# The split weights' slots, each begun at another byte phase of a partition's 512 bytes

## The reference

```python
x = x + 0.5 * swiglu_ffn(rmsnorm(x, ffn1_norm), ffn1_w_in, ffn1_w_out)   # 2048 -> 2*5504 -> 2048
h = rmsnorm(x, mix_norm)
qa, ka, va, qb, kb, vb, f_pre = split(h @ w_in)                          # 2048 -> 6152
out_a = dilated_attention(rmsnorm(qa), rmsnorm(ka), va, rel_bias_table)  # 8 heads of 128
out_b = forgetting_attention(rmsnorm(qb), rmsnorm(kb), vb, log_f)        # 8 heads of 128
x = x + concat(out_a, out_b) @ w_out
x = x + 0.5 * swiglu_ffn(rmsnorm(x, ffn2_norm), ffn2_w_in, ffn2_w_out)

def swiglu_ffn(x, w_in, w_out):
    gate, up = split(x @ w_in, 2)
    return (silu(gate) * up) @ w_out
```

## Time and profile before

| | |
|---|---|
| median of 2 runs | 1900.01 us (1899.78 to 1900.24) |
| the profiled execution | 1897.12 us |
| its span, first to last instruction | 1895.3 us |
| mean granted TensorE clock | 0.995 of full speed |
| PE busy | 1858.9 us, 98% of the span |
| weight load (PEld) busy | 1545.2 us, 82% |
| DVE busy | 946.6 us, 50% |
| ACT busy | 818.2 us, 43% |
| DMA | 343.70 MB read, 183 GB/s over the span |

### The profile page before, as it was taken

How to read it: one execution, slowest core, us unless ns; L and a number is a source line. 1 busy time by engine, 2 the same in 40 slices (tenths; PEclk the granted TensorE clock), 3 DMA queues, 4 the chain that set the end, 5 groups by cost and what they waited for, 6 DMA issues and landing times.

```text
span 1895.3 us, 20376 instructions
## 1 busy us (share of the span) xinstructions
PE 1858.9 (98%) x8470; PEld 1545.2 (82%) x8470; DVE 946.6 (50%) x1051; ACT 818.2 (43%) x971; POOL 26.9 (1%) x37
## 2 busy tenths in 40 slices
PE   6999999999999999999999999999999999999999
PEld 5888888888988888877777788888888888988887
DVE  4444444454544554365555555545444444444443
ACT  5444444444434444344444445444444444433332
POOL 1000000000000000000000000000000000000000
PEclk9999999999999999899999999999999999999999
DMA  6655555555655557344454455555655555556553
GB/s 225 213 197 181 197 185 192 190 187 172 206 194 186 181 200 241 108 137 156 145 166 155 164 170 177 180 198 179 198 180 199 182 195 180 192 185 210 202 202 116
DMA packets 175643, 347.13 MB, mean 183 GB/s; under 512 B 5808, under 2 KB 14064, under 8 KB 175424
## 3 DMA queue, kind: packets, MB, share of 16 engines
q1 hardware_dynamic: 172304, 337.92, 54.1%
q10 hardware_dynamic: 2080, 3.94, 0.6%
q0 software_dynamic: 1168, 3.97, 0.5%
HBM read 343.70 MB, written 3.68 MB: 183 GB/s over the span
## 4 chain that ended last, share of the span: by engine, by line
PE 93%; DVE 3%; ACT 2%; issue 1%; DMA 1%; ACTq 0%; DVEq 0%
PE acc L248 30%; PE acc L250 30%; PE acc L249 29%; ACT whi L458 2%; DVE wlo L676 1%; PE aux L275 1%; DMA x<-x 1%; PE aux L265 1%; PE aux L327 0%; DVE act_f L782 0%; PE aux L378 0%; PE aux L370 0%; PE aux L369 0%; PE aux L340 0%; PE aux L339 0%
## 5 line engine op out<-in xcount | busy, mean ns | idle before, releaser
L676 DVE TENSOR_TENSOR wlo<-raw,whi 128x1024 fp32r<-128x1024 f32 (+1 forms) x656 | 790.8, 1206 | 913.5 <-ACT whi L458 911.7
L458 ACT ACTIVATE whi<-raw 128x1024 fp32r<-128x1024 f32 (+1 forms) x656 | 684.6, 1044 | 1036.6 <-PE acc L250 1036.6
L248 PE MATMUL acc<-whi,xs 128*128 128x512 f32 (+1 forms) x1792 | 700.1, 391 | 3.7 <-DVE wlo L676 3.6
L250 PE MATMUL acc<-whi,xs 128*128 128x512 f32 (+1 forms) x1792 | 692.3, 386 | 0.0
L249 PE MATMUL acc<-wlo,xs 128*128 128x512 f32 (+1 forms) x1792 | 691.8, 386 | 0.0
L248 PEld LDWEIGHTS acc<-whi,xs 128*128 128x128 f32 x1792 | 337.4, 188 | 68.4 <-issue 5.1
L250 PEld LDWEIGHTS acc<-whi,xs 128*128 128x128 f32 x1792 | 337.3, 188 | 66.3
L249 PEld LDWEIGHTS acc<-wlo,xs 128*128 128x128 f32 x1792 | 337.6, 188 | 63.7
L248 PE MATMUL acc<-whi,act 128*128 128x512 f32 x688 | 268.1, 390 | 0.0
L250 PE MATMUL acc<-whi,act 128*128 128x512 f32 x688 | 267.7, 389 | 0.0
L249 PE MATMUL acc<-wlo,act 128*128 128x512 f32 x688 | 267.7, 389 | 0.0
(11 more groups left out here) (116 smaller groups left out, 519.4 us busy)
## 6 DMA issues: line engine op xcount, KB each, us to landing
raw<-ffn_w_in SPq DMA_DIRECT2D x160, 1024.0 KB, 4.9
raw<-ffn_w_out SPq DMA_DIRECT2D x80, 1024.0 KB, 4.9
raw<-w_in SPq DMA_DIRECT2D x48, 1024.0 KB, 5.0
raw<-w_out SPq DMA_DIRECT2D x16, 1024.0 KB, 4.9
raw<-ffn_w_in SPq DMA_DIRECT2D x16, 768.0 KB, 4.3
raw<-ffn_w_out SPq DMA_DIRECT2D x8, 768.0 KB, 4.3
x<-x ACTq DMA_DIRECT2D x4, 512.0 KB, 13.4
bias_vectors<-bias_vector POOLq DMA_DIRECT2D x1, 1536.0 KB, 9.0
```

Source lines behind the costliest of these rows:

```text
L248: mm(banks[b][:, 0:w], stationary[:, k, 0, tok], hi, start=k == 0, stop=False, skip_group_check=True)
L250: last = mm(banks[b][:, 0:w], stationary[:, k, 1, tok], hi, start=False, stop=k == k_total - 1, skip_group_check=True)
L458: A(whi[:, h % SLOTS, 0:n_el], raw[:, slot, first:first + n_el], ACT.Copy).then_inc(weights_hi, 1)
L676: V.tensor_tensor(wlo[:, h % SLOTS, 0:n_el], raw[:, slot, first:first + n_el], whi[:, h % SLOTS, 0:n_el].bitcast(f32), ALU.subtract).then_ ...
```

## The change

The two tensors `whi` and `wlo` of four slots become two rings, each 512 bytes longer, with four slots in each that overlap nowhere. A slot still holds 1024 elements (4096 bytes), but it begins later by a number of elements of its own. In bytes past a multiple of 512: the high parts of slots 0 to 3 begin at 16, 32, 64 and 256, the low parts at 8, 384, 480 and 496. The second weight tile of a half lies 2048 bytes behind the first (1536 where it is 384 wide), so it has the same phase. The start of the first tensor and of `arena` is rounded up to 512 and no longer to 1024; with that everything in front of the rings (`x`, `xs`, `raw`) moves down by 512 bytes, and what comes behind them moves too, all by multiples of 512. `wf`, `wf_hi`, `wf_lo` and `one_hot` keep their 32 bytes past a multiple of 512.

No instruction, operand shape, wait, semaphore or DMA is added, removed or moved on any engine; only addresses differ.

```diff
+HI_PHASE = (4, 8, 16, 64)
+LO_PHASE = (2, 96, 120, 124)
...
-        place = [-(-nc.sbuf_base // 1024) * 1024]
+        place = [-(-nc.sbuf_base // 512) * 512]
...
-        whi = sb("whi", [P, SLOTS, 2 * W], f32r)
-        wlo = sb("wlo", [P, SLOTS, 2 * W], f32r)
+        hi_ring = sb("hi_ring", [P, SLOTS * 2 * W + P], f32r)
+        lo_ring = sb("lo_ring", [P, SLOTS * 2 * W + P], f32r)
+        whi = [hi_ring[:, s * 2 * W + HI_PHASE[s]:(s + 1) * 2 * W + HI_PHASE[s]] for s in range(SLOTS)]
+        wlo = [lo_ring[:, s * 2 * W + LO_PHASE[s]:(s + 1) * 2 * W + LO_PHASE[s]] for s in range(SLOTS)]
...
-        place[0] = -(-place[0] // 1024) * 1024
+        place[0] = -(-place[0] // 512) * 512
...
-                    hi, lo = whi[:, slot, i * w:(i + 1) * w], wlo[:, slot, i * w:(i + 1) * w]
+                    hi, lo = whi[slot][:, i * w:(i + 1) * w], wlo[slot][:, i * w:(i + 1) * w]
...
-                A(whi[:, h % SLOTS, 0:n_el], raw[:, slot, first:first + n_el], ACT.Copy).then_inc(weights_hi, 1)
+                A(whi[h % SLOTS][:, 0:n_el], raw[:, slot, first:first + n_el], ACT.Copy).then_inc(weights_hi, 1)
...
-                V.tensor_tensor(wlo[:, h % SLOTS, 0:n_el], raw[:, slot, first:first + n_el],
-                                whi[:, h % SLOTS, 0:n_el].bitcast(f32), ALU.subtract).then_inc(weights_lo, 1)
+                V.tensor_tensor(wlo[h % SLOTS][:, 0:n_el], raw[:, slot, first:first + n_el],
+                                whi[h % SLOTS][:, 0:n_el].bitcast(f32), ALU.subtract).then_inc(weights_lo, 1)
```

## The result

The changed kernel takes 1934.93 us (1934.75 to 1935.11, 2 runs) against 1900.01: +34.9 us, a ratio of 1.0184 with a 95% interval of 1.014 to 1.0228. So it is slower, by about 2%; the interval reaches to both sides of that mark. The forecast was 1900 with 1892 to 1912, and is wrong. The profiled execution took 1934.75 us with a span of 1932.9, 37.6 more than before.

What follows compares the result with a forecast made beforehand. The prediction took PE's matmul pace, 226.7 ns for 512 columns, to bound the kernel. All four terms (moving operand, splits, DMA and layout, mixer) were 0, so it forecast 1900 us, the median before, with a range of 1892 to 1912.

Steps and rivals of the forecast that it cites:

- What bounds the kernel: Whole kernel: PE, busy 1858.9 of 1895.3 us and 93% of the wait chain, mostly the three products.
- the pricing rule: PE: any change to the matmul pace is paid in full, up to 7,824 times; changes to splits are mostly covered.
- The moving operand's start, PE: Three product lines: new start phases of the moving operand cost nothing, taken as 0; bounds +136 and -105 us.
- the `one_hot` pair: Plain float32 product, moving operand 32 bytes past a multiple of 512: claimed to show no phase cost within 0.01 us.
- The comparisons at multiples of 512: Second weight tile of 384-wide blocks and token block 1: even starts showed moves by 512 bytes to be free.
- The splits, DMA and the arena: ACT and DVE splits, DMA, stationary operands and moved layout: no cost, taken 0; doubled slot 0 splits at most 5 us.
- Rival A: Product streams: an off-boundary start costs fixed time per matmul, +9, +61 or +105 us; chances 0.07 over 2%, 0.04 between.
- point of decision: Rival over all slots: 4.9 ns a matmul, 38 us over 7,824, from which it decides the sign.
- middle band: Off-boundary start cost on the product streams, a slowdown between 0.6% and 2%; chance 0.04.
- Rival B: Slot 0's low part: the 8-byte phase halves its stream's pace, +136 us, 2036 us; chance 0.04.
- Rival C: Products: the fixed 13.4 ns is an equal-phase collision of both operands and would go, -105 us, 1795 us; chance 0.04.
- the fixed 13.4 ns: Each matmul on PE: the part of 226.7 ns beyond 213.3 ns, one cycle a column for 512 columns.

Runs made afterwards that it cites:

- stat32: Changed kernel with all ring slots back at multiples of 512 bytes and the stationary tensors 32 bytes past one; 1942.3 us (kernel before beside it 1899.7).
- both32: Changed kernel with all ring slots and the stationary tensors 32 bytes past a multiple of 512; 1901.5 us (kernel before beside it 1899.8).
- four_a: Changed kernel with slots 0 to 3 at 32, 64, 128 and 384 bytes, high and low parts alike; 1930.6 us (kernel before beside it 1899.7).
- u256: Changed kernel with all eight slots 256 bytes past a multiple of 512; 1901.7 us (kernel before beside it 1899.1).
- tiny: Changed kernel, same addresses, but from the fifth half on the splits handle only 8 of 1024 columns; 1903.1 us (kernel before beside it 1899.1).
- stag256: Changed kernel with slots at 0, 256 or 512 bytes, chosen differently for high and low parts; 1900.7 us, ratio 1.000 to the kernel before.
- u8: Changed kernel with all eight slots 8 bytes past a multiple of 512; 1940.7 us (kernel before beside it 1899.1).
- u16: Changed kernel with all eight slots 16 bytes past a multiple of 512; 1930.3 us (kernel before beside it 1899.1).
- pair3: Changed kernel with high parts at 256 and low parts at 496 bytes in all slots; 1945.6 us (kernel before beside it 1901.7).

## Why the prediction was wrong

**What bounds the kernel** was right, and so was the pricing rule: an effect on the pace of PE is paid nearly in full, over 7,824 matmuls (39.4 us of pace made 37.6 of span).

**"The moving operand's start, PE", taken at 0, is the step that failed.** It measured 5.2 ns a matmul, +38.7 us. I took 0 "because the only row with a phase shows 0", the `one_hot` pair. That row was true and did not carry over. By stat32 and both32 what matters is the difference to the stationary operand, and by the layout the pair even had one: `table`, its stationary operand, starts at a multiple of 512 and `one_hot` 32 bytes past one. But it was a single pair at two cycles a column, 384 columns wide, with a weight load of 8 columns, and the runs show that width and load change the price: at 384 columns 32 bytes are free at one cycle a column too (173.3 ns, slot 0 of four_a and stat32), at 512 they cost 6.6 ns. Which of these properties hid the cost in the pair wasn't tried. I had called the bound weak, and then gave it 0.81.

**The comparisons at multiples of 512** (the two token blocks, and the second weight tile of a 384-wide block) were right for what they tested, and u256 shows 256 bytes to be free as well, but they were blind to anything smaller.

**The splits, DMA and the arena** were right: the splits took 1061 and 1225 ns, in tiny the writes made no difference to the pace, and in stag256 the moved layout cost nothing.

**Rival A** had the sign, the engine and nearly the size (4.9 ns was its point of decision, 5.2 to 5.3 were measured), with 0.04 for its middle band, in which the 1.84% lie; no form of it that I priced gives them. Its mechanism, a fixed cost at the start of an off-boundary stream, is refuted by both32, where all streams start off the boundary and none pays. **Rival B** is refuted by u8 and u16: 8 bytes cost 5.7 ns and not 210. **Rival C** looked at the right pair of reads and had the sign wrong: equal phases are the best case that was found at 512 columns, not a collision.

The lines of 16 bytes that the Trainium skill gives (*SBUF — State Buffer*, "Specifications (TRN2)") don't explain it: whole lines of offset, 16 and 128 bytes, cost about as much as 8 bytes (231.7 and 232.4 against 232.4 ns). Another page of the Trainium skill, *TensorE: Matmul & The Clock Gate*, section "Step-by-step: what each phase is for", has TensorE read its two operands through two independent ports, so that loading the next weights takes no read bandwidth from the running matmul. stat32 and both32 show that the two are not independent in time: the pace of the moving stream depends on the address of the stationary operand, by 6.6 ns a matmul at 512 columns.

**What stays open.** The runs show that the pace depends on the difference of the operands' phases modulo 256 bytes, on the width of the matmul, on the length of the weight load, and on what ran before. They don't show the mechanism inside TensorE or SBUF, nor a rule that gives 2797, 2797, 2773 and 2759 from the eight phases, nor why slot 0 of u8 takes 2794 where the other slots, at the same phase, take 2787. Differences between 128 and 256 were tried only at 224 (480) and 240 (496). Nor is the fixed 13.4 ns explained; at 512 columns no run had a whole half below it.

## What to carry to other kernels

Where f32r matmuls of 512 columns run back to back, let the moving and the stationary operands start at the same byte phase within 256 bytes of a partition. Hand layouts and odd paddings (a 32-byte tensor ahead of a ring) can break it for a whole stream, here at 1.3 to 2.4% of the time, with nothing in the profile but a distance between matmul starts that is a few ns longer. At other widths, time the pace again: at 384 columns several of these phases were free. And a row bounds a cost only if it runs at the same pace, with the same width, and beside the same other reads; the nearest row in size need not be near in kind.

## What the hardware did that I had not expected

- Equal phases of TensorE's two operands give 226.7 ns for 512 f32r columns at 2.4 GHz; 32 bytes of difference in either direction (stat32, and slot 0 of four_a) give 233.
- One stream in three off phase costs as much as all (2784 against 2780 ns a half).
- With the same phases in every half, a stream can hold either of two paces, 2747 or 2820 ns a half (pair3), and change from one to the other where small products interrupt it.
- At 384 columns 32 bytes of difference cost nothing (stat32, 173.3 ns).
- At 512 columns, stationary operands of 32 columns, a load of 109 and not 188 ns, run slower (231.7 ns) than those of 128.
